# Moving the fifteenth expert's down product ahead of the sixteenth expert's up product in a two-layer decoder trunk

## The reference, cut to what matters

```python
def expert_block(args):
    tok, e = args
    xb = h[tok]                                   # up to 128 tokens of one expert
    return (jax.nn.silu(xb @ w_gate[e]) * (xb @ w_up[e])) @ w_down[e]
...
contrib = y.reshape(slots, D) * w_buf[:, None]
x = x + g2 * (sum of both chosen experts' contributions)
```

## Time and profile before

| | |
|---|---|
| median of 3 runs | 1489.31 us (1480.3, 1490.01, 1489.31) |
| the profiled execution | 1481.74 us |
| its span on the core | 1480.1 us |
| PE busy | 1373.5 us (93%) |
| DVE busy | 981.7 us (66%) |
| ACT busy | 727.3 us (49%) |
| POOL busy | 297.9 us (20%) |
| mean granted PE clock | 0.973 |
| DMA | 341.20 MB, 231 GB/s |

### The profile page before, as it was taken

One profiled execution on the slowest core, in us unless ns is written; L12 is line 12 of the kernel. 1 busy time (PEld: TensorE's weight loads), 2 busy tenths in 40 slices (PEclk: granted clock), 3 DMA queues, 4 the chain that ended last, 5 costly groups with the idle time before them and its releaser, 6 DMA issues.

```text
span 1480.1 us, 18790 instructions
## 1 busy us (share of the span) xinstructions
PE 1373.5 (93%) x7075; PEld 1086.3 (73%) x7076; DVE 981.7 (66%) x934; ACT 727.3 (49%) x776; POOL 297.9 (20%) x255
## 2 busy tenths in 40 slices
PE   3999999999999999999949999999998999999793
PEld 1766877666867888888748787788777888888482
DVE  4325575323577999999871667542757899999284
ACT  4324355122245777777742545522325777776160
POOL 1000000000014344544310000000013444445120
PEclk9999999999999999999979999999999999999897
DMA  9766402775676999999843130132364999999275
GB/s 301 276 217 226 155 1 86 243 268 199 219 281 225 361 380 388 391 372 378 291 125 114 57 115 1 58 114 95 105 246 169 338 372 377 378 377 384 95 255 190
DMA packets 157256, 341.20 MB, mean 231 GB/s; under 512 B 17150, under 2 KB 19394, under 8 KB 157186
## 3 DMA queue, kind: packets, MB, share of 16 engines
q1 hardware_dynamic: 141170, 316.97, 59.3%
q0 software_dynamic: 16016, 23.30, 4.7%
HBM read 350.68 MB, written 23.61 MB: 253 GB/s over the span
## 4 chain that ended last, share of the span: by engine, by line
PE 75%; DVE 9%; DMA 5%; ACT 4%; DVEq 3%; issue 2%; SPq 1%; POOL 0%; POOLq 0%; ACTq 0%
PE PS L1196 15%; PE PS L1198 14%; PE PS L1197 14%; PE PS L1594 7%; PE PS L1598 7%; PE PS L1590 7%; PE PS L1130 3%; DVE ring_parts L2206 2%; ACT reg L950 2%; PE PS L1578 2%; DMA ring<-in_w_up 2%; DMA y_rows<-reg,icur 1%; SPq L486 1%; PE PS L1603 1%; DMA ring<-in_w_ada 1%
## 5 line engine op out<-in xcount | busy, mean ns | idle before, releaser
L1196 PE MATMUL PS<-ring_parts 128*128 128x512 f32 (+1 forms) x704 | 275.6, 391 | 9.3 <-DVE hT_parts L1838 5.5
L2206 DVE TENSOR_TENSOR ring_parts<-ring,reg_parts 128x2048 fp32r<-128x2048 f32 x124 | 278.1, 2284 | 1.1 <-ACT reg_parts L1054 1.0
L1054 ACT ACTIVATE reg_parts<-ring 128x2048 fp32r<-128x2048 f32 x124 | 230.5, 1909 | 67.7 <-DMA ring<-in_w_down 35.2
L1830 DVE TENSOR_TENSOR ring_parts<-ring,ring_parts 128x2048 fp32r<-128x2048 f32 (+1 forms) x52 | 112.9, 2210 | 154.4 <-ACT ring_parts L872 154.4
L1196 PEld LDWEIGHTS PS<-ring_parts 128*128 128x128 f32 x704 | 132.7, 188 | 60.4 <-issue 27.6
L872 ACT ACTIVATE ring_parts<-ring 128x2048 fp32r<-128x2048 f32 (+1 forms) x52 | 93.4, 1845 | 152.1 <-DMA ring<-in_w_in 112.2
L2206 DVE TENSOR_TENSOR ring_parts<-ring,hT_parts 128x2048 fp32r<-128x2048 f32 x68 | 155.2, 2287 | 15.0 <-issue 13.5
L1198 PE MATMUL PS<-ring_parts 128*128 128x512 f32 x384 | 149.8, 390 | 0.0
L1197 PE MATMUL PS<-hT_parts,ring_parts 128*128 128x512 f32 x384 | 149.8, 390 | 0.0
L1054 ACT ACTIVATE hT_parts<-ring 128x2048 fp32r<-128x2048 f32 x68 | 126.5, 1909 | 13.2 <-DMA ring<-in_w_gate 7.2
L1598 PE MATMUL PS<-ring_parts,reg_parts 128*128 128x512 f32 x528 | 130.6, 389 | 0.0
(11 more groups left out here) (328 smaller groups left out, 2392.4 us busy)
## 6 DMA issues: line engine op xcount, KB each, us to landing
ring<-in_w_up SPq DMA_DIRECT2D x32, 2048.0 KB
ring<-in_w_gate SPq DMA_DIRECT2D x32, 2048.0 KB, 11.9
ring<-in_w_down SPq DMA_DIRECT2D x32, 2048.0 KB
ring<-in_w_ada SPq DMA_DIRECT2D x40, 1024.0 KB, 5.4
ring<-in_w_in SPq DMA_DIRECT2D x16, 2048.0 KB, 7.9
ring<-in_w_ada SPq DMA_DIRECT2D x4, 2048.0 KB, 12.3
ring<-in_w_out SPq DMA_DIRECT2D x4, 2048.0 KB, 9.9
reg<-y_rows SPq DMA_DIRECT2D x16, 512.0 KB, 6.3
```

The source lines that it names most:

```text
L1054: act.activation(high[:, cols], ring[:, 3 * k + part, cols], ACT.Copy).then_inc(w_hi[part], 1)
L1196: pe.matmul(out_, left[0], right[0], start=first, stop=False)
L1830: tt(ring_r[:, unit_slot(n), cols], w, ring_r[:, 2 + n % 2, cols].bitcast(F32), ALU.subtract).then_inc(lo_done, 1)
L2206: tt(ring_r[:, 3 * k + part, cols], ring[:, 3 * k + part, cols], high[:, cols].bitcast(F32), ALU.subtract).then_inc(w_lo[part], 1)
```

## The change

In the last step PE's order changes from gate(15), transposes(14), up(15), down(14) to transposes(14), gate(15), down(14), up(15). DVE's end begins with `finish(14)` instead of having it behind the low parts of expert 15's down weights. Nothing else changes; ACT's, POOL's and SP's programs are the same. The change is in both layers.

```diff
@@ PE, after the loop over expert steps
-                step(E - 1, E // 2 - 1, 1, more=False)
+                transposed_act(E - 2, 0)
+                pe.wait_ge(silu_done, at(silu_done, l, E - 1))
+                gate_product(E - 1, 1)
+                down(E - 2, 0)
+                second_product(E - 1, 1)
+                overflow(E - 1, E // 2 - 1, 1, E)
                 transposed_act(E - 1, 1, gu_free)
                 last_down(1).then_inc(d_ready, 1)
@@ DVE, after the loop over expert steps
+                dve.wait_ge(y_stored[0], at(y_stored[0], l, 16 * (E // 2 - 1)))
+                finish(E - 2, 0)
                 hidden(E - 1, 1)
                 overflow(E - 1)
                 weights_low(E - 1, 1, 2, w_high[0])
-                dve.wait_ge(y_stored[0], at(y_stored[0], l, 16 * (E // 2 - 1)))
-                finish(E - 2, 0)
                 hidden_low(E - 1)
```

## The result

| | before | after |
|---|---|---|
| median of 16 runs each | 1484.7 us | 1499.95 us |
| lowest and highest | 1480.3 and 1490.41 | 1493.97 and 1507.58 |
| profiled execution, its span | 1481.74, 1480.1 us | 1503.29, 1501.6 us |
| PE busy | 1373.5 us (93%) | 1386.8 us (92%) |
| DVE busy | 981.7 us (66%) | 981.7 us (65%) |

The ratio is 1.0101, with a 95% interval of 1.0084 to 1.0118: 12.5 to 17.5 us slower. The median of the kernel before over 16 runs is lower than that of its first three. The profiled execution of the kernel after lies in the upper part of its 16 runs.

What follows compares the result with a forecast made beforehand. PE, busy for 93% of the span, was taken as the bound, with a serial tail behind its last work. Layer 1's +7.4 us and layer 0's +8.0 summed to +15.4, giving 1501 us between two base levels, range 1490 to 1510.

Steps and rivals of the forecast that it cites:

- Points 1 and 2: PE's last step: transposes(14) cost nothing by moving; PE idles 5.4 us (layer 1) and 6.4 (layer 0) before down(14).
- Points 3 and 4: From up(15) to the last down product: 6.6 us and 1.35 us of lost cover, 7.95 us later in each layer.
- point 4: Last down product: PE waits 1.35 us for the low parts of expert 15's down weights, formerly made beside down(14).
- Point 5: Layer ends: earlier finish(14) lets expert 15's scatter run without loads beside it, giving back 3.46 (layer 1) and 2.82 us.
- The narrow cover in layer 0: Tail of layer 0: DVE's additions of the lower rows end 10.6 us behind finish(15)'s start, before the higher rows' about 11.7.
- Point 6: Down(14): the idle stretch lowers PE's clock, costing 2.9 us a layer, 5.8 together; bounds 0 and 5.5.
- the fall that I had priced it from: Earlier stretch of the trace: clock 0.53 after 3.44 us idle before 1405.13, back 5.8 us after work began.
- over 8 us at 0.50: Sign named for the clock's fall: down(14)'s 24 matmuls take over 8 us at a granted clock of 0.50.
- The sum: Both layers: 7.4 us in layer 1 and 8.0 in layer 0, together +15.4 us, +1.04%, forecast 1501 us.
- B: Rival for down(14): the clock holds or is back at once, so +9.6 us; chance 0.15.
- C: Rival before down(14): DVE's low part comes when PE asks; idle 2 us, +1.1 and +0.7 us, 1483.5; chance 0.07.
- D: Rival in the last step: a second clock fall, or the scatter stays slow; +21 us, 1503 to 1510; chance 0.15.

Runs made afterwards that it cites:

- transposes_first: Kernel before with only the four transposes of expert 14's activations moved ahead of expert 15's gate product; +0.3 us, ratio 1.0003.
- dve_only: Kernel before with only DVE's new end, finish(14) ahead of hidden(15), and PE's old order; +2.2 us, ratio 1.0014.
- late_early: up_low_late plus the low parts of expert 15's down weights moved ahead of hidden(15) on DVE; +7.0 us against the kernel before, ratio 1.0039.
- up_low_late: Whole change plus the low parts of expert 15's up weights moved behind hidden_low(14) on DVE; +11.2 us against the kernel before, ratio 1.0066.
- pe_only: Kernel before with only PE's new order, DVE's end as before; +25.1 us, ratio 1.0162.
- spare22: Whole change plus 22 unused matmuls between expert 15's gate product and down(14); +9.6 us against the kernel before, ratio 1.0067.
- spare: Whole change plus 40 unused matmuls between expert 15's gate product and down(14); +14.9 us against the kernel before, ratio 1.0085.

## Why the prediction was right

The forecast was 1501 us and +1.04%; measured were 1499.95 and +1.01%. The mechanism was right at every step, one term, the clock, was put at 5.8 us where 3.5 were measured, and the closeness of the two totals is partly luck. Point by point:

- **Points 1 and 2, transposes and idle.** Right. Down(14) started with DVE's low part, behind idle of 5.12 and 5.96 us where 5.4 and 6.4 had been worked out (from start to start, so with the end of the last matmul in them); the transposes are free (transposes_first).
- **Points 3 and 4, the lost cover.** Right: without the clock's 1.40 and 2.14 us, S is 9.25 - 1.40 = 7.85 us longer in layer 0 and 10.08 - 2.14 = 7.94 in layer 1, where 7.95 had been forecast for both. The difference in point 4 is 1460.05 - 1458.74 = 1.31 us, not 1.35; the trace has 1477.10 - 1473.88 - 1.92 = 1.30. Dve_only has that wait and the trip through DVE without the rest, with finish(14) added to the trip (3.5 us in all); late_early removes the wait. Up_low_late shows that in layer 1 DVE's order is what down(14) waits for; in layer 0 this is read from the timeline alone.
- **Point 5, the tail.** Right: the scatter took 3.40 and 4.41 us where 3.35 and 4.38 had been taken, and T shrank by 3.57 and 2.72 where 3.46 and 2.82 had been forecast. That it agrees to 0.1 us is luck, since the same scatter beside loads varies by a microsecond from one execution to the next (7.20 and 8.27 in layer 0). Pe_only shows that the early evacuation earns it. The narrow cover in layer 0 held: the lower rows' additions ended at 760.58 + 4.87 = 765.45, the higher rows' began at 766.14.
- **Point 6, the clock.** The mechanism was right and the size was not: 1.40 and 2.14 us instead of 2.9 each. The fall was there in both layers, but the clock was back 3.0 and 4.8 us after work had begun again (granted clock 0.53 from 735 to 736 and 0.51 from 1462 to 1463, 1.00 behind both), against 5.8 in the fall that I had priced it from. So down(14) took 6.98 and 7.85 us at a mean clock of 0.78 and 0.69, not over 8 us at 0.50 as I had named for a sign. Spare22 confirms that work in the idle stretch removes the fall.
- **The sum.** By the traces the change costs 13.0 us, not 15.4; the oversized clock, 5.8 - 3.5, makes 2.3 of the difference. That the medians differ by 15.3, as forecast, is partly chance: their interval holds both figures. So is the 1501: I took the first executions for two levels and put the base midway, at 1485.5. The 16 runs fill the space between 1480.3 and 1490.41 without two levels, but their median, 1484.7, is close to that middle.
- **The rivals.** B (+9.6) lies outside the interval of the timed difference. Spare22 is about what B would have looked like, at +9.6. C fell with the first wait seen; up_low_late brought about its condition in layer 1, where the sum is +2.8 us, or +1.15 without the 1.62 of the clock, as C had it (+1.1). So it was still not free. Of D the second fall occurs in some executions (spare22's layer 0, dve_only's layer 1), but it cost only 0.2 us each time, since most of it lies beside DVE's low parts.

## What to carry to other kernels

Before two products change places, ask what the first of them covers. Here down(14)'s operand came from DVE, which had no gap, so down(14) could not start earlier, and the time that the up product had filled became idle time. A gain further on, here 6.3 us from a scatter that no longer ran beside loads, has to be set against it, and with PE's new order it came only with the evacuation moved too (pe_only). A fine balance is best read in stretches between fixed instructions, since whole executions of the same kernel differ here by 10 us (1480.3 to 1490.41).

## What the hardware showed unexpectedly

- The granted clock fell to 0.50 behind an idle of only 1.90 us in up_low_late, 1.3 us after PE had begun again, and stayed at 1.00 behind the same idle in late_early. In dve_only and spare22 it fell near the last down product, where gaps of 0.8 to 2.0 us stand close together. So a low stretch isn't a fixed price of an edit: down(14) took from 5.57 to 8.09 us (the longest in pe_only's layer 1), so it cost from nothing to 2.5 us.
- Expert 15's indirect scatter took 3.4 us in layer 1 where the four loads of 512 KB had landed before it (after), 6.8 where they were issued 3.6 us ahead of it (before), and 8.9 where they were issued 0.84 us ahead (pe_only). In between lies dve_only, 4.3 us with the loads 5.4 us ahead. Even with the loads long ahead it isn't fixed: 4.1 and 4.2 us in spare and late_early. Layer 0 has the same order: 4.4 (after), 7.2 with the loads 2.5 us ahead (before), and 10.2 with them 0.04 us ahead (pe_only).
